# Exponents in planes, the last output tiles between projection units, pool products in three places, merge halves moved

## The reference, cut to what matters

```python
def step(s, inp):
    qc, kc, vc, gc = inp
    cum = jnp.cumsum(gc.astype(jnp.float32), axis=1)
    inter = jnp.einsum("blhk,bhkv->blhv", qc * jnp.exp(cum), s)
    diff = cum[:, :, None] - cum[:, None, :]
    decay = jnp.exp(jnp.where(mask[None, :, :, None, None], diff, -jnp.inf))
    att = jnp.einsum("bihk,bjhk,bijhk->bhij", qc, kc, decay)
    intra = jnp.einsum("bhij,bjhv->bihv", att, vc)
...
o_gla = rms_norm(y_gla, gla_norm) * jax.nn.silu(f["r"]).reshape(b, t, GLA_HEADS, GLA_DV)
...
return o @ w_out
```

```python
for l in range(DEPTH_2):
    h = rmsnorm(h_res, norm_gain[l])
    proj = h @ w_in[l]
    u_pool, z_pool, c_q, c_kv, k_rope, z_mla, g_pool, g_mla = jnp.split(proj, IN_SPLIT_POINTS, axis=-1)
    y_pool = (pool_mix(u_pool, pool_w_group[l], pool_scale[l]) * jax.nn.silu(z_pool)) @ pool_w_up[l]
    o_mla = mla(c_q, c_kv, k_rope, pos, ...)
    y_mla = (o_mla * jax.nn.silu(z_mla)) @ mla_w_up[l]
    merged = jax.nn.sigmoid(g_pool) * y_pool + jax.nn.sigmoid(g_mla) * y_mla
    h_res = h_res + merged @ w_out[l]
```

## Time and profile before

| | us |
|---|---|
| median of 3 runs | 3729.84 (3727.48 to 3732.07) |
| profiled execution, its own time | 3728.76 |
| span of its core | 3727.0 |

### The profile page before, as it was taken

The page is one execution under the profiler, slowest core; times in us unless marked ns, Lnnn a source line. Parts: engine busy times, 40 slices in busy tenths (PEclk is TensorE's granted clock), DMA queues, the critical chain, the costliest instruction groups (busy, mean ns, idle before and its releaser), DMA issues.

```text
span 3727.0 us, 51106 instructions
## 1 busy us (share of the span) xinstructions
PE 3390.9 (91%) x20406; PEld 2828.4 (76%) x20406; DVE 1958.8 (53%) x2838; ACT 1435.2 (39%) x2196; POOL 218.7 (6%) x225
## 2 busy tenths in 40 slices
PE   1998776579999999999998999999999989999998
PEld 1776444457778877889855679999998557799998
DVE  6647577865534443446564544454446545444433
ACT  2532455344432333234345443343343444433322
POOL 1000033210000000000020000000000100000000
PEclk9999877569999999999999989999999989899999
DMA  5562101013333224223200002343432000023333
GB/s 194 182 201 93 51 15 59 10 55 113 108 118 117 90 94 164 94 88 121 81 1 29 24 24 83 106 140 92 136 113 76 1 29 24 30 86 109 113 94 100
DMA packets 94493, 321.82 MB, mean 86 GB/s; under 512 B 10352, under 2 KB 11632, under 8 KB 93488
## 3 DMA queue, kind: packets, MB, share of 16 engines
q1 hardware_dynamic: 76224, 249.66, 20.6%
q0 software_dynamic: 17312, 67.78, 5.2%
q10 hardware_dynamic: 720, 1.12, 0.1%
HBM read 295.38 MB, written 23.20 MB: 85 GB/s over the span
## 4 chain that ended last, share of the span: by engine, by line
PE 80%; DVE 12%; ACT 5%; DMA 1%; issue 1%; DVEq 0%; POOL 0%; ACTq 0%; SPq 0%; POOLq 0%
PE psum L146 76%; DVE mixer L171 4%; PE psum L149 3%; DVE mixer L181 2%; DVE wlo L171 1%; DVE arena L194 1%; DVE arena L171 1%; DVE junk L185 1%; ACT arena L155 1%; DVE mixer L198 1%; DVE region L171 1%; ACT whi L163 1%; ACT arena L163 0%; DMA stage<-in_wm 0%; ACT L155 0%
## 5 line engine op out<-in xcount | busy, mean ns | idle before, releaser
L146 PE MATMUL psum<-region,whi 128*128 128x260 f32 (+2 forms) x8896 | 1909.8, 312 | 22.8 <-DVE region L171 18.4
L146 PEld LDWEIGHTS psum<-region,whi 128*128 128x128 f32 (+1 forms) x8896 | 1444.1, 188 | 134.3 <-DVE region L171 16.8
L146 PE MATMUL psum<-region,wlo 128*128 128x260 f32 (+2 forms) x4448 | 1380.8, 310 | 0.0
L171 DVE TENSOR_TENSOR wlo<-stage,whi 128x1024 fp32r<-128x1024 f32 (+2 forms) x454 | 512.9, 1130 | 732.2 <-ACT whi L163 697.3
L146 PEld LDWEIGHTS psum<-region,wlo 128*128 128x128 f32 (+1 forms) x4448 | 839.7, 189 | 49.2
L163 ACT CAST whi<-stage 128x1024 fp32r<-128x1024 f32 (+2 forms) x454 | 441.7, 973 | 271.2 <-PE psum L146 177.7
L146 PE MATMUL psum<-arena 128*128 128x65 f32 (+8 forms) x2064 | 423.6, 356 | 2.8 <-ACT arena L155 1.2
L163 ACT COPY arena<-psum 128x512 f32<-128x512 f32 (+10 forms) x428 | 190.4, 445 | 416.3 <-PE psum L146 382.2
L146 PE MATMUL psum<-mixer 64*128 64x128 f32 (+6 forms) x1140 | 230.5, 446 | 121.0 <-DVE mixer L198 55.0
L146 PEld LDWEIGHTS psum<-arena 128*128 128x128 f32 (+4 forms) x2064 | 256.6, 181 | 100.3 <-issue 90.8
L154 ACT ACTIVATE arena<-psum 128x260 f32<-128x260 f32 (+1 forms) x236 | 101.0, 428 | 596.0 <-PE psum L146 595.6
(11 more groups left out here) (144 smaller groups left out, 2771.5 us busy)
## 6 DMA issues: line engine op xcount, KB each, us to landing
stage<-in_w SPq DMA_DIRECT2D x144, 512.0 KB, 3.5
stage<-in_wi SPq DMA_DIRECT2D x55, 512.0 KB, 4.2
stage<-in_wm SPq DMA_DIRECT2D x48, 512.0 KB, 3.4
stage<-in_wo SPq DMA_DIRECT2D x48, 512.0 KB, 3.5
stage<-in_wg SPq DMA_DIRECT2D x44, 512.0 KB, 3.3
stage<-in_wu SPq DMA_DIRECT2D x44, 512.0 KB, 3.3
stage<-in_wd SPq DMA_DIRECT2D x32, 512.0 KB, 3.3
arena<-xr_scratch POOLq DMA_DIRECT2D x7, 2080.0 KB, 8.8
```

What stands on the lines that cost most here:

```text
L146: return Issued(self, self.e and self.e.matmul(out, w, x, start=start, stop=stop, skip_group_check=True))
L171: return Issued(self, e and e.tensor_tensor(out, a, b, op))
```

## The change

Levels: `dd` is laid out as four planes of 256 in each slot (k forward, q backward, q forward, k backward), and for Bs > 1 one subtraction of 512 elements makes a direction's two planes; the sign of k goes into the exponential (`scale=-1.0`), which is two instructions, for q (`dq`) and k (`dk`). For Bs = 1 only the two q planes are made and the pair product takes k itself. Behind level 31's subtractions ScalarE, and in round 32 VectorE, convert the weights for the second wo unit.

Tail: products 4 to 7 follow wo units 0 to 3 and turns 4 to 7 follow units 2 to 5, through `OUT0`; wo's first chunk uses banks 0 and 1, the turns 2 and 3. `rt` has own places for tiles 6 and 7. The load of x waits for turn 7.

Layers: ScalarE calls `half_now` for the second half ahead of the first half's last unit (n == 12), the other engines behind it. The pool products are `pe_pg` and `act_pg`: group 0 ahead of the last tile's turns, 1 behind it, 2 and 3 behind the second score item; the weights of pg + 1 to pg + 4 are converted behind item `PER`. The halves 0 to 3 of the merged tile stand ahead of the last gate's and up's steps (k, z = 7, 1), and `cuts` lets the first output unit run both chunks over k tiles 0 to 3 and then 4 to 7. Some buffers move to other regions.

```diff
@@ pe_gemm
-        for ci, (b, free) in enumerate(bs):
...
+        for ka, kb in zip(cuts or (0, nk), (cuts or (0, nk))[1:]):
+            for ci, (b, free) in enumerate(bs):
...
+                for k in range(ka, kb):
@@ mixer
-    dd, qe = at(28928, 2, 2, 512), at(30976, 2, 2, 512)
+    dd, qe = at(28928, 2, 1024), at(30976, 2, 2, 512)
-    rt = at(35072, 2, 512)
+    rt = [at((35072, 35584)[j % 2], 512) for j in range(6)] + [at(3368, 512), at(8488, 512)]
+    def q_planes(s, Bs):
+        return dd[:, s, 256:768].rearrange("p (two g b) -> p g two b", two=2, b=Bs)
+    def planes_of(s, d, Bs):
+        return dd[:, s, :].rearrange("p (two d n) -> p two d n", two=2, d=2)[:, :, d, :].rearrange(
+            "p two (g b) -> p g two b", b=Bs)
@@ pe_gla
-        for j in (4, 5, 6):
-            pe_yo(e, j)
-        pe_turn(e, 4)
-        pe_yo(e, 7)
-        pe_turn(e, 5)
@@ act_round, act_gla
+        if r == NL:
+            e.wait_ge(*D["dd", NL - 1])
+            act_weights(e, W, W.last["wo", 0, 0] + 1)
-                e.activation(dd[:, n % 2], dd[:, n % 2], ACT.Exp).then_inc(*A.up("dd", n))
+                x = dd[:, n % 2, 256:768]
+                e.activation(x, x, ACT.Exp).then_inc(*A.up("dq", n))
+                if Bs > 1:
+                    x = k_planes(n % 2, 256)
+                    e.activation(x, x, ACT.Exp, scale=-1.0).then_inc(*A.up("dk", n))
@@ dve_round, dve_gla
+        if r == NL + 1:
+            dve_weights(e, W, W.last["wo", 0, 0])
-                e.tensor_tensor(dq[:, :, 1, :], cfv[:, :, 1, :], rf_, ALU.subtract).then_inc(*D.up())
-                e.tensor_tensor(dk[:, :, 0, :], rf_, cfv[:, :, 0, :], ALU.subtract).then_inc(*D.up())
-                e.tensor_tensor(dq[:, :, 0, :], cbv[:, :, 0, :], rb_, ALU.subtract).then_inc(*D.up())
-                e.tensor_tensor(dk[:, :, 1, :], rb_, cbv[:, :, 1, :], ALU.subtract).then_inc(*D.up("dd", n))
+                if Bs > 1:
+                    for d, c in ((0, cf), (1, cb)):
+                        ref = c[:, :, 0, Bs - 1:Bs] if d == 0 else c[:, :, 1, 0:1]
+                        e.tensor_tensor(planes_of(sl_, d, Bs), c, ref[:, :, None, :].broadcast_to([128, n_g, 2, Bs]),
+                                        ALU.subtract).then_inc(*(D.up("dd", n) if d else D.up()))
+                else:
+                    q = q_planes(sl_, 1)
+                    e.tensor_tensor(q[:, :, 1, :], cf[:, :, 1, :], cf[:, :, 0, :], ALU.subtract).then_inc(*D.up())
+                    e.tensor_tensor(q[:, :, 0, :], cb[:, :, 0, :], cb[:, :, 1, :], ALU.subtract).then_inc(*D.up("dd", n))
-            elif s == 1 and Bs:
+            elif s == 1 and Bs > 1:
@@ pool_gla
-                e.tensor_tensor(qe[:, sl_, 0, :], dd[:, sl_, 0, :], ql, ALU.mult).then_inc(*G.up("qs", n))
+                e.tensor_tensor(by_halves(qe[:, sl_, 0, :], Bs), q_planes(sl_, Bs), by_halves(ql, Bs),
+                                ALU.mult).then_inc(*G.up("qs", n))
@@ the projection's lists
+    for m in range(6):
+        OUT0[m] += [("output", "turn", m + 2)] * (m >= 2) + [("output", "product", m + 4)] * (m < 4)
@@ pool_out
-        e.wait_ge(*K.sgla.pe["yo", 7])
+        e.wait_ge(*K.sgla.pe["turn", 7])
@@ rounds
+            if (n, half, q) == (12, 0, "act"):
+                half_now(e, q, h_second[l])
             do(key, i)
...
-            half_now(e, q, h_second[l])
+            if q != "act":
+                half_now(e, q, h_second[l])
@@ pe_att
+            if (s, t) == (1, NTB - 1):
+                pe_pg(e, l, (0,))
...
+        pe_pg(e, l, (1,))
         bs.flush()
...
+                if it == 1:
+                    pe_pg(e, l, (2, 3))
@@ act_att
-        act_weights(e, W, W.last["pg", l] + 2)
...
-        act_weights(e, W, W.last["pg", l] + 4)
...
+                if it == 1:
+                    act_pg(e, l, (2, 3))
+                if it == PER:
+                    act_weights(e, W, W.last["pg", l] + 4)
@@ dve_att
-        dve_weights(e, W, W.last["pg", l] + 4)
...
+                if it == PER:
+                    dve_weights(e, W, W.last["pg", l] + 4)
@@ beside2
-            out += n_in1[0].steps(3, 3, 2)
+            out += n_in1[0].steps(8, 6, 4)
@@ pe_lay2, act_lay2
-                    lambda ci, k_: (cut(m.yh, k_, ci), cut(m.yl, k_, ci), g(k_)), 2, HC, T, D)
+                    lambda ci, k_: (cut(m.yh, k_, ci), cut(m.yl, k_, ci), g(k_)), 2, HC, T, D, cuts=(0, 4, 8) if k == 0 else None)
+                if (k, z) == (7, 1):
+                    half_now(e, "act", h_mg[l][half], 0, 4)
@@ dve_lay2
+                if (k, z) == (7, 1):
+                    half_now(e, "dve", h_mg[l][half], 0, 4)
                 key = ("up", l, half, k, z)
                 dve_weights(e, W, W.last[key] + 2)
-                if (k, z) == (7, 1):
-                    bs.flush()
-                    half_now(e, "dve", h_mg[l][half], 0, 4)
```

More of the change, by code:

```diff
@@ L337, in dve_weights, with pe_gemm @@
         e.tensor_tensor(lo, W.staged(u), hi.bitcast(F32), ALU.subtract).then_inc(*W.lo.up(u))
-def pe_gemm(e, W, bank, psum, key, name, units, rhs, nch, N, done, count, M=128, each=False):
-    bs = [bank.take((key, ci), count, key, ci) for ci in range(nch)]
+def pe_gemm(e, W, bank, psum, key, name, units, rhs, nch, N, done, count, M=128, among=range(8), each=False, cuts=None):
+    bs = [bank.take((key, ci), count, key, ci, among=among) for ci in range(nch)]
     k0 = UNITS[name][units[0]][0]
@@ L486, in mixer @@
     gin, gin2 = K.sig("gate_weights"), K.sig("levels_in")
-    rd = [K.sig(f"r_in{i}") for i in range(2)]
+    rd = [K.sig(f"r_in{i}") for i in range(4)]
+    rd = [rd[i] for i in (0, 1, 0, 1, 0, 1, 2, 3)]
     K.yd = [K.sig(f"y_in{i}") for i in range(2)]
@@ L1452, in pe_turn @@
         T, A, D = sgla.pe, sgla.act, sgla.dve
-        b, free = bank.take(("turn", j), D, "out", j, among=(6, 7) if j < 4 else (0, 1))
+        b, free = bank.take(("turn", j), D, "out", j, among=(6, 7) if j < 4 else (2, 3))
         for x in free:
@@ L2310, in rounds @@
         if half == 0:
-            while any(s[0] == "sc" and s[1].key in (("in", 0, 1), ("next", 1, 1)) for s in bs.todo):
-                bs.tick()
-            half_now(e, q, h_second[l])
+            assert not any(s[0] == "sc" and s[1].key in (("in", 0, 1), ("next", 1, 1)) for s in bs.todo)
+            if q != "act":
+                half_now(e, q, h_second[l])
             bs.todo += lora_steps(l, 0)
@@ L2358, in do @@
                         e.wait_ge(*sffn.pe["root", ("in", 0, 0), 1])
+                    if key[0] == "kr" and l == 0:
+                        e.wait_ge(*sffn.dve["add", ("end", 1), 7])
                     e.wait_ge(*T[key, ci])
@@ L2426, in beside_pairs, with pe_pg, act_pg @@
             bs.tick()
+    PG_COLS = ((0, 348), (348, 694), (694, L2))
+    def pe_pg(e, l, groups):
+        S, m = slay[l], M[l]
+        T, A, D = S.pe, S.act, S.dve
+        if groups[0] == 0:
+            u = W.take(("pg", l), f"pg_{l}", 0, True, T, "pgu")
+            e.wait_ge(*W.land[u % W.NS][u])
+        wp = W.staged(W.last["pg", l]).rearrange("p (g n) -> p g n", g=4)
+        for g in groups:
+            e.wait_ge(*D["mixed", g])
+            for c, (c0, c1) in enumerate(PG_COLS):
+                b, free = bank.take(("pg", l, g, c), A, "pg", g, c, among=range(8) if g < 2 else SUM_BANKS)
+                for f in free:
+                    e.wait_ge(*f)
+                e.matmul(psum[:, b, 0:c1 - c0], wp[:, g, :], m.upl[:, g, c0:c1], True, True).then_inc(*T.up("pg", g, c))
+        if groups[-1] == 3:
+            T.mark("pgu")
+    def act_pg(e, l, groups):
+        S, m = slay[l], M[l]
+        T, A = S.pe, S.act
+        for g in groups:
+            for c, (c0, c1) in enumerate(PG_COLS):
+                e.wait_ge(*T["pg", g, c])
+                e.activation(m.upl[:, g, c0:c1], psum[:, bank.of["pg", l, g, c], 0:c1 - c0], ACT.Copy,
+                             scale=P[f"ps_{l}"][:, g:g + 1]).then_inc(*A.up("pg", g, c))
     def pe_att(e, bs, l):
```

149 lines of the change are left out of this document (64 added, 85 removed).

## The result

The changed kernel takes 3685.39 us (median of 4 runs, 3680.89 to 3688.44) against 3728.66 (4 runs, 3726.88 to 3732.07) of the kernel before: ratio 0.988, 95% interval 0.9866 to 0.9894. The forecast was 3690, a gain of 39.8 us; 43.3 were gained.

The account below looks back on a forecast made before the run. TensorE, busy 91% of the span, was taken as the bound, with VectorE setting the levels' pace. −13.4 − 11.5 + 7.6 + 2.0 − 24.4 = −39.7 gave 3690 us; own range 3681 to 3699, with rivals 3664 to 3708.

Parts of the forecast that it names:

- The levels: GLA levels: subtractions and exponential in planes, no k product at block size 1; 13.4 us less.
- D: Levels: GpSimd's product in planes takes 2.2 us, costing 12.4 on 20 VectorE-bound levels; 3702; chance 10%.
- F: Levels: GpSimd's product takes 3.6 us or more and 20 levels wait; at 4.0, +48.4, 3738; chance 5%.
- The tail: Last tiles' products interleaved with output gemm units: 12.5 less, 1.0 back for the clock's rise; 11.5 us less.
- Rival C: Tail: the clock falls in the interleaved products, as in the 30.3 us before; +12, 3702; chance 12%.
- The seams: Each layer's input gemm: next weights' high cast queues behind eight casts, so TensorE starts later; +3.8 a layer, 7.6.
- Rival B: Seams and attention item 18: the added waits don't occur because queues have the casts ready earlier; 3667; chance 13%.
- Pool products in three places: Attention: 6.65 us less at the start, 7.65 more at item 18; net +1.0 a layer, +2.0.
- The merges: Four merge places: early halves and cut first output unit, the unit taking 6.1 us; 24.4 us less.
- Rival E: Merges: the halves find VectorE or ScalarE busy and half of that gain is lost; 3702; chance 6%.
- G: The change doesn't do what it says: wo units still start after products, or halves form where they were; 3715; 2%.
- At nothing: Three-step norm, buffers that change region and the new waits on them: no effect on the time.

Follow-up runs that it names:

- the conversions spread: Changed kernel with the four gate weight conversions put one behind each of attention items 18, 22, 26 and 30: 3688.53 us, ratio 0.989.
- the kernels with early weights: Changed kernel with gate weights converted outside the attention items: 3674.52 us; with high cast in front at seams too: 3658.17; that with only one unit early: 3657.06.

## Why the prediction was right

**The levels** (13.4 forecast): 13.6 by undoing them. With the 30.3 us of products that left this stretch, 43.7 were forecast and 44.02 measured. The rows of VectorE, 0.69 for 128x512 and none for the dropped k product, carried over, and GpSimd's product, for which no row of a plane pattern existed, took 1.27 to 1.29, so the value taken was the lower bound and rivals D and F (10% and 5%) did not occur. Block size 1 takes 1.40 to 1.41. By the Trainium skill (GPSIMD Engine Reference, section 7 "Performance pitfalls for Q7 kernels"), reads with a wide step would make it some 1.9, an estimate from that page; the measurement decides, and it is a tenth more here and not half. The Trainium skill's other rule (SBUF — State Buffer, section "SBUF: two separate sides") is borne out once more: two subtractions beside the long GpSimd products take 3.45 instead of 1.42.

```profile
652.61 3.45 DVE L171 TENSOR_TENSOR mixer<-hold 128x512 f32<-128x512 f32 x2
```

**The tail** (11.5 forecast, 13.5 measured: 30.3 against 16.75): the term that was mis-sized is the clock's rise, put at 1.0 us of cost. The projection's first unit runs from 789.15 to 794.82, 5.67 us, against 6.5 in the kernel before: the clock is up when it starts, and 0.8 is gained instead of 1.0 lost. It was at 0.50 up to 787, during the last levels' products, and is at 1.00 in the microsecond ahead of the start, in which TensorE is idle:

```profile
784.00:787.00 3.00, 2.96 (x28) 2.96 (x30) 2.67 (x3) 1.44 (x2) 0.00 (x0) 0.50 0.00 0
788.00:789.00 1.00, 0.00 (x0) 0.00 (x0) 1.00 (x1) 0.00 (x0) 0.00 (x0) 1.00 0.24 37
```

The products are 4.19 and 4.20 as forecast. Rival C did not occur, but it was a near one: in a row, behind the same first unit, the third and fourth product had the lower clock. The row that I set against it (4.54 at 773.23) was misread: that product stands behind a level's products and not between gemm units.

**The seams** (3.8 each forecast, 3.15 and 3.50 measured): the chain was right and the wait longer than its upper bound. I had TensorE start 4.3 later than before; it starts 5.19 and 4.84 later, since the eight casts take 5.76 and not 5.6, and VectorE starts 0.56 after the end of the high cast, where I had allowed next to nothing (behind the fourth cast at item 18 it is 0.09, so this is no fixed price). Of that, 2.04 and 1.34 come back behind the seam, which I had put at 0.5 for another reason. Most of it is the granted clock. In the kernel before it is at 0.50 for some 6 us behind the wait of 2.05, with TensorE full; in the changed kernel it falls during the idle time of 7.24 and is at 1.00 again from 1747 on, 5 us after TensorE's start. First before, then after:

```profile
1768.00:1774.00 6.00, 6.00 (x26) 5.65 (x27) 3.26 (x4) 2.06 (x3) 0.00 (x0) 0.50 0.18 59
1747.00:1753.00 6.00, 5.79 (x46) 5.58 (x47) 1.93 (x2) 2.00 (x4) 0.57 (x1) 1.00 0.53 183
```

Rival B fell for this place.

**Pool products in three places** (+1.0 each forecast; +1.00 and −0.65 measured): the start gained 4.88 and 4.46 for 5.0, and the waits at item 18 are 4.88 + 2.20 = 7.1 us, the forecast's "some 7". The net is smaller than the jump of several us that these parts show with nothing changed in them, so its agreement in layer 0 is luck as much as proof. Behind the first turn of probabilities the part is 5.9 and 3.8 us longer, where the forecast had 7.65 − 1.65 = 6.0. The order of the losses and gains is shown by their rows and by the kernels with early weights, and rival B did not occur here either. What the chain had wrong is the weight of the transfer: it does hold up the fourth cast by 2.43, but with the conversions spread and no such wait the two parts were only 2.3 us shorter.

**The merges** (24.4 forecast, 22.9 between the two traces, 24.0 in the four places by undoing them): the first output unit does not run at TensorE's pace throughout. VectorE forms halves 4 to 7 in 3.12 us from 2386.11 on, and TensorE takes one each 0.80:

```profile
2386.11 3.12 DVE L171 TENSOR_TENSOR region<-arena,region 128x520 fp32r<-128x520 f32 x4
```

That makes the unit 7.39 us long (2383.78 to 2391.17) and not 6.1. Half of this miss is made up because I had also taken the old unit too short: in layer 0's first half it ran to 2420.85 and not to 2420.20. Rival E did not occur: the first four halves are ready when TensorE starts the unit. Nor did G, by the rows of the tail and of the unit.

**At nothing**: undoing the norm's steps shows nothing. The moved regions and the later load of x were not undone; the stretch behind the load of x in which no other edit stands, from the norm behind the first chunk to kr, is 870.9 us before and 870.7 after.

The misses, as gains: +2.0 in the tail, −1.5 in the merges, +1.0 at the seams, +1.65 in layer 1's attention (inside its jump), +0.3 in the levels and +0.5 ahead of them make 3.95 of the 4.0 us between 39.7 and 43.7. That the sum comes out to 4 us is in part luck: the two attention parts alone jump by more than that with the clock, and only one profile of each kernel is compared.

## What to carry to other kernels

When a block of work is moved ahead on one engine's queue, list what that queue still owes to others and put the short item that another engine waits for in front of the block: here one cast of 1.04 us ahead of eight was worth 15.8 us over two seams. A conversion put into a loop in which every engine is nearly last cost about its length here, packed at one place or spread over four; look for room outside the loop. And cut the consumer (`cuts`) when half of its input is made early, since early input alone gave little over half. In counting what a wait of TensorE costs, look at the granted clock behind it as well: a wait of 1.46 us cost 2.4 to 2.9.

## What the runs showed of the hardware that was not expected

TensorE's granted clock was down from 1.00 to 0.51 of 2.4 GHz with TensorE busy throughout (7.00 of 7.00 us), after two products of 24 matmuls in a row and an idle gap of 0.87 us; the same products, one at a time between gemm units, stayed at 1.00. It fell in the same way, with TensorE busy again, behind waits of 1.46 (first output unit), 2.05 (the seam before) and 1.97 us (the norm); behind the last it fell in some profiles and not in others with the same instructions, and that is the jump of 1.5 us there.

And with the same instructions up to that point, the first level's product came at 642.5 to 648.4 us after the start of the span. The executions of one kernel lie 2.4 to 14.6 us apart, so that a part worth 3 us shows in its stretch and hardly in a median.
